# Start addresses of the moving tiles: 60 tiles spread over the remainders by 128 bytes

## The reference, cut to what matters

```python
# block 1
z = rmsnorm(x) @ w_in                       # 1024 -> 2752 columns, then four mixers
x = x + rmsnorm(concat(y_a, y_b, y_c, y_d) @ w_out)
gate, up = split(rmsnorm(x) @ ffn_w_up)     # 1024 -> 2 * 2816
x = x + rmsnorm((gelu(conv3(gate)) * up) @ ffn_w_down)   # 2816 -> 1024
# block 2
x = x + 0.5 * (silu(h @ w_gate1) * (h @ w_up1)) @ w_down1
x = x + hybrid_mixer(rmsnorm(x))            # w_in 1024 -> 3088, w_out 1024 -> 1024
x = x + 0.5 * (silu(h @ w_gate2) * (h @ w_up2)) @ w_down2
return rmsnorm(x)
```

## Time and profile before

| | |
|---|---|
| device time, median of 3 runs (lowest, highest) | 1670.56 us (1664.17, 1672.58) |
| device time of the profiled execution | 1664.33 us |
| span of the profiled execution, first to last instruction | 1662.6 us |
| PE matmul busy | 1627.3 us, 98% |
| PE weight loads busy (beside the matmuls) | 1317.7 us, 79% |
| DVE, ACT, POOL busy | 812.3, 683.5, 266.8 us |
| mean granted TensorE clock | 0.995 of full |
| HBM read | 146.03 MB, 89 GB/s over the span |

### The profile page before, as it was taken

The page is one execution under the profiler, slowest core; times in us unless marked ns, Lnnn a source line. Parts: engine busy times, 40 slices in busy tenths (PEclk is TensorE's granted clock), DMA queues, the critical chain, the costliest instruction groups (busy, mean ns, idle before and its releaser), DMA issues.

```text
span 1662.6 us, 22061 instructions
## 1 busy us (share of the span) xinstructions
PE 1627.3 (98%) x8640; PEld 1317.7 (79%) x8640; DVE 812.3 (49%) x1342; ACT 683.5 (41%) x1228; POOL 266.8 (16%) x225
## 2 busy tenths in 40 slices
PE   9999999999999999999999999999999999999997
PEld 6776777777888888868888888877877888888887
DVE  5567445465655542364444433357365444444333
ACT  7555556445434433344333332345133433333222
POOL 1231111102222210002222210000020032223000
PEclk9999999999999999999999999999999999999999
DMA  5221100313333333314232333332122323322332
GB/s 196 80 90 40 40 26 26 116 63 102 101 102 101 90 91 104 96 51 124 92 101 91 100 92 94 106 99 94 60 89 89 101 91 100 102 90 85 105 101 76
DMA packets 45982, 149.56 MB, mean 90 GB/s; under 512 B 5260, under 2 KB 8500, under 8 KB 45880
## 3 DMA queue, kind: packets, MB, share of 16 engines
q1 hardware_dynamic: 41760, 142.10, 27.2%
q10 hardware_dynamic: 4120, 6.06, 1.1%
HBM read 146.03 MB, written 2.11 MB: 89 GB/s over the span
## 4 chain that ended last, share of the span: by engine, by line
PE 91%; DVE 4%; ACT 3%; issue 1%; DMA 1%; POOL 0%; DVEq 0%; SPq 0%; ACTq 0%; POOLq 0%
PE bank L257 90%; PE bank L378 1%; DMA raw<-in_w_in 1%; ACT hi L995 0%; DVE lo L1664 0%; ACT sq L1014 0%; PE bank L438 0%; DVE acc L1680 0%; PE bank L430 0%; DVE x L2123 0%; DMA raw<-in_w_out 0%; ACT L1025 0%; DVE yf L2119 0%; DVE hs L2365 0%; DVE B L2287 0%
## 5 line engine op out<-in xcount | busy, mean ns | idle before, releaser
L1664 DVE TENSOR_TENSOR lo<-raw,hi 128x512 fp32r<-128x512 f32 (+1 forms) x514 | 392.3, 787 | 603.8 <-ACT hi L995 603.6
L257 PE MATMUL bank<-xh,hi 128*128 128x512 f32 x1576 | 613.1, 396 | 7.2 <-issue 2.2
L257 PE MATMUL bank<-xh,lo 128*128 128x512 f32 x1576 | 604.0, 390 | 1.3 <-DVE lo L1664 1.3
L257 PE MATMUL bank<-xl,hi 128*128 128x512 f32 x1576 | 596.7, 390 | 0.0
L995 ACT ACTIVATE hi<-raw 128x512 fp32r<-128x512 f32 (+1 forms) x540 | 321.9, 616 | 460.3 <-PE bank L257 413.2
L257 PEld LDWEIGHTS bank<-xh,hi 128*128 128x128 f32 x1576 | 296.4, 188 | 80.0 <-issue 11.0
L257 PEld LDWEIGHTS bank<-xh,lo 128*128 128x128 f32 x1576 | 296.8, 188 | 64.4 <-DVE lo L1664 2.1
L257 PEld LDWEIGHTS bank<-xl,hi 128*128 128x128 f32 x1576 | 296.8, 188 | 63.5 <-issue 3.1
L257 PE MATMUL bank<-fH,hi 128*128 128x512 f32 (+1 forms) x550 | 210.1, 382 | 0.0
L257 PE MATMUL bank<-fH,lo 128*128 128x512 f32 (+1 forms) x550 | 209.3, 381 | 0.0
L257 PE MATMUL bank<-fL,hi 128*128 128x512 f32 (+1 forms) x550 | 209.3, 381 | 0.0
(11 more groups left out here) (392 smaller groups left out, 1114.9 us busy)
## 6 DMA issues: line engine op xcount, KB each, us to landing
raw<-in_ffn_w_up SPq DMA_DIRECT2D x88, 512.0 KB, 3.5
raw<-in_w_in SPq DMA_DIRECT2D x50, 512.0 KB, 3.4
raw<-in_ffn_w_down SPq DMA_DIRECT2D x48, 512.0 KB, 3.5
raw<-in_ffn_w_gate SPq DMA_DIRECT2D x44, 512.0 KB, 3.4
raw<-in_ffn_w_down SPq DMA_DIRECT2D x24, 384.0 KB, 3.1
raw<-in_w_out SPq DMA_DIRECT2D x16, 512.0 KB, 3.5
x<-in_xt SPq DMA_DIRECT2D x8, 256.0 KB, 5.9
x<-in_xt ACTq DMA_DIRECT2D x8, 256.0 KB, 5.1
```

The lines of the kernel that those rows point to most:

```text
L257: return pe.matmul(out, w, x, start=start, stop=stop, skip_group_check=True)
L1664: dve.tensor_tensor(k.lo[i % CUT][:, 0:w], k.raw[u % RAW][:, at:at + w], k.hi[i % CUT][:, 0:w].bitcast(F), SUB).then_inc(k.cut_tail[i % 2], 1)
```

## The change

Only start addresses change. The sixteen tiles `xh` and `xl` become windows in one tensor `split`: window n begins `REMAINDERS[n]` words after a multiple of 2048 bytes, even n are `xh`, odd n are `xl`. The remainders in words of 4 bytes are 1, 3, 5, 7, 10, 15, 20, 28 for `xh` and 2, 4, 6, 8, 12, 16, 24, 31 for `xl`. The 22 `fH` are windows in a tensor with 640 words for each, window n beginning n words in (0 to 21), and the 22 `fL` likewise at n + 10 words (10 to 31). That makes 16 + 44 = 60 tiles. `split` takes 33280 bytes and `fH` and `fL` 56320 bytes each, all multiples of 128, so every other tile keeps its remainder: `hi` and `lo` stay at 0, `cA` at 64, though most lie at other addresses than before. No instruction is added, removed or moved, and none has another shape; in the profile the names `xh` and `xl` become `split`.

```diff
+REMAINDERS = (1, 2, 3, 4, 5, 6, 7, 8, 10, 12, 15, 16, 20, 24, 28, 31)
...
-        k.xh = [new("xh", T, R)[:, :] for _ in range(8)]
-        k.xl = [new("xl", T, R)[:, :] for _ in range(8)]
+        split = new("split", 16 * T + 128, R)
+        starts = [n * T + REMAINDERS[n] for n in range(16)]
+        k.xh = [split[:, at:at + T] for at in starts[0::2]]
+        k.xl = [split[:, at:at + T] for at in starts[1::2]]
...
-                S.fH = [made("fH", T, R)[:, :] for _ in range(22)]
-                S.fL = [made("fL", T, R)[:, :] for _ in range(22)]
+                heads, tails = made("fH", 22 * 640, R), made("fL", 22 * 640, R)
+                S.fH = [heads[:, 640 * n + n:640 * n + n + T] for n in range(22)]
+                S.fL = [tails[:, 640 * n + n + 10:640 * n + n + 10 + T] for n in range(22)]
```

## The result

The changed kernel takes 1695.28 us (median of 4 runs, 1692.8 to 1696.29) against 1667.57 us of before on the same chip: 1.0162 times as long, 95% interval 1.0138 to 1.0187, 27 to 28 us. The span of its profiled execution is 1691.0 us, 28.4 us more.

A forecast was written before the change was run, and what follows sets the result against it. PE's matmul pace was taken to bound the kernel. The profiled 1664.3 us plus 2.5 for moving reads, all else 0, gave 1666.8, or 1673 against the median; own range 1664 to 1681, stated range 1636 to 1712.

The forecast's parts named there:

- What bounds the kernel: Whole kernel: PE is busy 98% and makes 91% of the chain, so its pace goes almost whole into the time.
- Writes by DVE and ACT: Writes to tiles with shifted starts: taken to cost 0; if ACT's cost a tenth more, 7 us on an idle engine.
- POOL's tails: L2583, 66 pieces: a shift costs between -0.20 and +0.12 us each, at most 8 us, hidden; zero in the sum.
- PE's moving reads: Matmuls streaming shifted tiles: an extra fetch on the 2992 at odd words, +2.5 us in all.
- the least that a split pair could cost: PE fetching words in pairs: a run beginning mid-pair needs 257 pairs instead of 256, +0.83 ns a matmul.
- rival A: PE's moving reads: a start off a boundary costs each matmul a restart, +8 to +84 us; chance 0.20.
- the two signs of being wrong: PE's moving reads: granularity above two words paid at both ends, or the 13.3 ns hanging on the two addresses.
- Rival B: PE's moving reads: odd words stream at one word per 0.83 ns, +598 us, about 2270; chance 0.06.
- Rival C: PE's stream colliding with the next weights' read: spread starts avoid some, -35 us for half, -70 for all; chance 0.16.
- the 13.3 ns: Each large PE matmul at full clock: the part of its 226.7 ns that is not its columns.

The follow-up runs named there:

- (0, 32): Inputs at word 0, weights moved to word 32, counted by 256 bytes, against the kernel before: 232.4 ns a matmul; that kernel 1.0152 times before.
- the sets above: Three sets of follow-up kernels that moved only start words of moving tiles and weights, measured against the kernel before; ratios from 1.0009 to 1.0360.
- (8, 4): Stage C's gated tiles at word 8, weights at 4, counted by 256 bytes, against the kernel before: 226.8 ns; that kernel 1.0150 times before.
- (1, 0): Inputs at word 1, weights at 0, counted by 256 bytes, against the kernel before: 237.8 ns a matmul; that kernel 1.0336 times before.

## Why the prediction was right or wrong

**What bounds the kernel**: right. The loss is PE's pace and goes almost whole into the time.

**Writes by DVE and ACT, POOL's tails**: right, nothing in the time. POOL's own pieces did change, by the -0.20 us that was the lower bound: 1.09 us where `fH` and `fL` both begin at word 1 or 2, 1.29 at 0, 4, 8 or 16, off PE's path.

**PE's moving reads**: the step that failed. I took "the least that a split pair could cost", 0.83 ns on the 2992 matmuls at odd words. Measured were 5.0 ns in the mean, on even words as well: tiles at word 4 take 236 ns and at 20 and 24 they take 231 and 235, while 7 is nearly free. The term of +2.5 us is +28. The time lies outside the forecast's own range of 1664 to 1681, and beyond the 8 us that I had set for a difference; for slower than that I had given 0.26. The stated range up to 1712 held 1695 only because it took in the cheaper part of rival A, so its success says nothing for the forecast's mechanism. Of the two signs of being wrong that I had named, the second came: the surplus over the columns hangs on the two addresses.

**Rival A**, a start off a boundary is dear: the size was in its span of +8 to +84 us, its mechanism is only half of it. In the equal places a boundary of 32 bytes shows. But a tile at a perfect boundary is slowed when only the weights move (0, 32). The reading by which an odd start should pay for a lone word does not fit either: tiles at 8 or 48 against weights at 16, or at 16 or 40 against weights at 8, have no lone word in their lines and pay 6.5 ns. The 16-byte lines of the Trainium skill, SBUF — State Buffer, section "Specifications (TRN2)", do not give these numbers by themselves.

**Rival B**, half pace at odd words: did not occur; at full clock no steady distance in any kernel was over 245 ns.

**Rival C**, a quarrel with the weight load: nearer to the mechanism than the forecast, and with the wrong sign. The pace does hang on where the weights lie. But the placement of before was already the best kind, and the spread could only lose. Two of my arguments against it were unsound. The first, that a stream of another pace passes every relative position anyway: the sets above refute it. The second was the row with weights at remainder 64 and the same distance. It was a single load, followed by a two-pass matmul; in the nearest steady case, tile at 0 and weights at 16 words, the distance is 233.3. One row of a transition is no measurement of a steady state. The Trainium skill, TensorE: Matmul & The Clock Gate, "Step-by-step: what each phase is for", which spoke against C with two independent read ports, is not borne out here as far as pace goes: with the inputs left at 0, moving the weights by 128 bytes made their matmuls 5.5 ns longer.

What stays open: why. That two reads of the same memory meet is the reading that fits best. It is argued, not shown: no run had a float32r stream without weight loads beside it. At half clock no difference appears. The timeline of the changed kernel there, with the starts three matmuls apart:

```profile
301.06 0.63 PE L257 MATMUL bank<-split,lo 128*128 128x512 f32 x1
301.49 1.05 PE L257 MATMUL bank<-split,hi 128*128 128x512 f32 x2
302.34 0.63 PE L257 MATMUL bank<-split,lo 128*128 128x512 f32 x1
```

1.28 / 3 = 0.427 us, as before, at words where full clock shows the spread. In the half-clock stretches of the other kernels the steady distances are 426 or 427 ns as well; only in one stretch with the inputs spread and `xl` 128 bytes on do they alternate between 423 and 430, with nearly the same mean. So the loss takes the fast stream. Open too are the rule behind (8, 4), the places not tried, the influence of the neighbour, and whether the 13.3 ns that remain at the best places have the same source.

## What to carry to other kernels

Where PE streams float32r tiles back to back at full clock, the start addresses of moving tiles and weights are part of the kernel: keep both at multiples of 256 bytes, or else at equal places by 256 that are multiples of 32 bytes (0, 32, 64 and 128 were measured), and pay with padding; the worst uniform placement measured here costs 3.4 to 3.6% of the whole kernel. An edit that changes a tensor's size moves everything allocated after it, so compare addresses before explaining a difference. And to learn a pace, count starts in a window of the steady state and do not rely on a single transition.

## What was not expected of the hardware

- The distance between starts depends on moving and stationary address together, by 256 bytes: 226.9 ns at the best, 237.8 at one word, up to 245 for single pairs.
- In the changed kernel it repeats from unit to unit: over 39 units of stage A's up projection 99% of the distances lie within 1 ns of their place's median. It is not so everywhere: at (1, 0) 63% do and at (0, 32) 62%, so there a mean over many units is needed.
- Matmuls of 256 columns hardly react: 119.8 ns before, 118.7 after, 117.3 to 122.0 in the other kernels, the most with `fH` at word 1 and weights at 0, where 512 columns lose some 9 ns.
- DVE and ACT are indifferent to the starts tried, 746 against 748 ns and 633 against 633. POOL is not: its subtraction L2583 took 1287 ns in the median before and 1093 with `fH` and `fL` at word 1.
